# Router, slot table and experts in one block, with expert 0's turned rows from a matrix product

## The chip, the cores and the metric

The kernel runs on one core of a Trainium2 chip. The metric is device time in microseconds of one execution. Engines: PE (TensorE, with PEld for its weight loads), DVE (VectorE), ACT (ScalarE), POOL (GpSimd), SP (SyncE, which here only issues DMAs). All tiles are float32 unless said otherwise.

## The reference, cut to what matters

A first hybrid layer and a second one with latent attention and a recurrence run ahead of the part that matters here, and are not touched. They leave `h`, 512 tokens of 1024 numbers. Then comes a mixture of 32 experts:

```python
logits = (ht @ router_w + router_b)
top_val, top_idx = lax.top_k(logits, TOP_K)            # 4 of 32
gates = jax.nn.softmax(top_val, axis=-1)
# tokens sorted by expert into blocks of 128 slots
u = clamped_swiglu(h_pad[idx] @ w1[e] + b1[e])         # 1024 -> 2048 -> 1024
y = u @ w2[e] + b2[e]                                  # 1024 -> 1024
ffn = sum of a token's 4 rows y, each times its gate
x = layer_norm(DEEPNORM_ALPHA * x + (1 + gt2) * ffn, ln2_g, ln2_b)
```

## The kernel before, in words

The kernel is written engine by engine: a block holds one list of instructions for each engine, the engines meet only at semaphores, and all of them meet at the end of a block. Within an engine the order is that of the code.

`mixed` (L2992) first runs `joined`, which makes `h` (tile `h_mix`, tokens on partitions), stores it to DRAM as `h_rows`, and leaves the router's logits in PSUM bank 6. Then come three blocks.

Block "router" (L3043). POOL clears semaphores, writes zeros and id tiles (L3057 to L3060). SP stores the zeros to the slot table `slot_tokens` in DRAM and issues the first six weight chunks (1 MB each) of expert 0. DVE adds the bias, finds the top four experts of each token, builds a one-hot tile with 16 small comparisons (L3102) and sums it to `member` (L3104). ACT takes the exponentials (L3080). PE counts with 14 products (L3068 to L3071) how many earlier tokens chose the same expert: `rank`. DVE meanwhile weighs the gates (L3107 to L3112). Then (L3115 to L3136) it turns ranks into slot numbers `token_slots`: token of rank r in expert e gets slot 128e + r, and those beyond 128 go to extra blocks. L3139 to L3145 make the plan of these extra blocks.

Block "fill_slots" (L3152). POOL writes token numbers to the slot table with 16 indirect DMAs (L3159), one for each tile of 128 tokens and each choice. PE turns the gates (L3166), ACT makes the diagonals of the last gate (L3172) and copies the turned gates (L3175).

Block "experts" (L3195). For each block of slots POOL's `fetch` (L3329, L3334) loads 128 token numbers and gathers those rows of `h_rows` into `h_mix[:, 0]`. PE turns them (L3363), ACT copies the high part (`high_rows`, L3574) and DVE the low part (`low_rows`, L3481). Weights come in chunks of 128 x 2048, 8 for the first layer and 4 for the second. SP loads them into a ring of six slots; ACT makes the high part (`high`, L3565), DVE the low part (`low`, L3456), PE multiplies (L3382): three products for each piece. From chunk 4 on, `high` waits until PE has used the chunk four before it. SP loads a chunk when `low` has freed its slot. `swiglu` on DVE (L3463 to L3475) and `sigmoid` on ACT (L3569) make `u`. Expert 0's first layer has a part of its own before the loops; PE then turns expert 1's rows and `u`, and the loop over experts 1 to 31 follows, in which the first layer of expert i, the turning of rows i+1 and the second layer of i alternate. SP loads the bias row of the next expert (L3265) between chunks 3 and 4. At the end POOL gathers the four rows of each token, and PE, DVE, ACT and POOL make the output. The extra-block part of each loop is read from the plan with `value_load` after the loop.

Of the kernel before, what the change touches and what calls it, by code (L numbers as in the profile page):

```python
# [13 lines left out]
ALU = mybir.AluOpType  # L14
# [8 lines left out]
P = 128  # L23
SEQ = 512
# [1844 lines left out]
def hybrid_then_moe(nc, A, out):  # L1869
    with ExitStack() as ctx:  # L1870
# [40 lines left out]
        with ExitStack() as inner:  # L1911
            h_rows, slot_tok = mixed(c, A, h, part, inner, gates, slots, plan, vec, gates_T, bias2, gate_diag)
        experts(c, A, h, h_rows, slot_tok, bias_rows, plan, Y, gates, slots, vec, out, gates_T, bias2, gate_diag)


# [1076 lines left out]
def mixed(c, A, h, part, ctx, gates, slots, plan, final, gates_T, bias2, gate_diag):  # L2992

    nc = c.nc

    def sb(name, shape, dt=F32):
        return ctx.enter_context(nc.sbuf_tensor(name, shape, dt))

    h_rows = nc.dram_tensor("h_rows", [SEQ, D], F32).ap()

    slot_tok = nc.dram_tensor("slot_tokens", [SLOTS + CAP, 1], I32).ap()
    hT = sb("hT2", [P, DT, SEQ])
    rw = sb("router_w", [P, DT, E])
    rb = sb("router_b", [P, E])
    c.far.close()
    with nc.sbuf_tensor("leave_rows", [P, 5, D], F32) as vec:
# [10 lines left out]

    logits = sb("logits", [P, TT, E])
    top = sb("top_values", [P, TT, 8])
    top_i = sb("top_indices", [P, TT, 8], U32)  # L3020
    top_f = sb("top_index_f", [P, TT, 8])
    neg = sb("neg_top", [P, TT])
    total = sb("gate_total", [P, TT])
    e_int = sb("expert_ids_i", [P, E], I32)
    e_id = sb("expert_ids", [P, E])
    hot = sb("one_hot", [P, TT, TOPK, E])
    gated_hot = sb("gated_hot", [P, TT, TOPK, E])
    dense = sb("gates_by_expert", [P, TT, E])
    member = sb("member", [P, TT, E])
    rank = sb("rank", [P, TT, E])  # L3030
    count = sb("expert_count", [P, E])
    extra = sb("extra_blocks", [P, 2, E])
    cum = sb("extra_cum", [P, E])
    first = sb("extra_first", [P, E])
    over = sb("over_capacity", [P, TT, E])
    dest = sb("dest", [P, TT, TOPK])
    token_id = sb("token_id", [P, TT], I32)
    blk_i = sb("block_ids_i", [1, EXTRA], I32)
    blk = sb("block_ids", [1, EXTRA])
    before_blk = sb("experts_before", [1, EXTRA, E])  # L3040
    plan_f = sb("plan_f", [1, 2 + EXTRA])
    zeros = sb("zero_ids", [SLOTS // CAP + 1, CAP], I32)
    with nc.Block("router") as block:  # L3043

        @block.sync
        def _(sp):
            sp.wait_ge(c.pool_ready.sem, c.pool_ready.at(1))
            sp.dma_start(slot_tok.rearrange("(b s) o -> b (s o)", s=CAP), zeros[:]).then_inc(c.stored.sem, 16)

            for ch in range(RAW):  # L3050
                load_expert_chunk(c, A, sp, 0, ch)
            sp.wait_ge(c.stored.sem, c.stored.at(1))

        @block.gpsimd
        def _(pool):
            nc.clear_and_free_semaphores(done_with)
            nc.gpsimd.memset(zeros[:], 0)  # L3057
            nc.gpsimd.iota(token_id[:], pattern=[[P, TT]], base=0, channel_multiplier=1)
            nc.gpsimd.iota(blk_i[:], pattern=[[1, EXTRA]], base=0, channel_multiplier=0)
            nc.gpsimd.iota(e_int[:], pattern=[[1, E]], base=0, channel_multiplier=0).then_inc(c.pool_ready.sem, 1)  # L3060

        @block.tensor
        def _(pe):
            pe.wait_ge(c.dve_done.sem, c.dve_done.at(2))
            for t in range(TT):
                out = c.banks[:, 1, t * E:(t + 1) * E]
                for b in range(t):
                    nc.tensor.matmul(out, c.ones[:], member[:, b, :], start=(b == 0), stop=False)  # L3068
                nc.tensor.matmul(out, c.upper_strict[:], member[:, t, :], start=(t == 0), stop=True)
            for b in range(TT):  # L3070
                last = nc.tensor.matmul(c.banks[:, 1, TT * E:(TT + 1) * E], c.ones[:], member[:, b, :], start=(b == 0),  # L3071
                                        stop=(b == TT - 1))
            last.then_inc(c.products.sem, 1)

        @block.scalar
        def _(act):

            act.wait_ge(c.dve_done.sem, c.dve_done.at(1))
            for t in range(TT):
                last = nc.scalar.activation(gates[:, t, :], top[:, t, 0:TOPK], ACT.Exp, bias=neg[:, t:t + 1],  # L3080
                                            accum_out=total[:, t:t + 1])
            last.then_inc(c.act_done.sem, 1)

        @block.vector
        def _(dve):
            dve.wait_ge(c.pool_ready.sem, c.pool_ready.at(1))
            nc.vector.tensor_copy(blk[:], blk_i[:])
            nc.vector.tensor_copy(e_id[:], e_int[:])

            c.dve(dve, nc.vector.tensor_tensor(logits[:], c.banks[:, 6, 0:TT * E].rearrange("p (t e) -> p t e", t=TT),  # L3090
                                               spread(rb[:], TT), ALU.add))
            for t in range(TT):
                last = nc.vector.max(top[:, t, :], logits[:, t, :])
            c.dve(dve, last)
            nc.vector.tensor_scalar(neg[:], top[:, :, 0], -1.0, None, ALU.mult).then_inc(c.dve_done.sem, 1)
            for t in range(TT):
                last = nc.vector.max_index(top_i[:, t, :], top[:, t, :], logits[:, t, :])
            c.dve(dve, last)
            c.dve(dve, nc.vector.tensor_copy(top_f[:], top_i[:]))
            for t in range(TT):  # L3100
                for k in range(TOPK):
                    last = nc.vector.tensor_scalar(hot[:, t, k, :], e_id[:], top_f[:, t, k:k + 1], None, ALU.is_equal)  # L3102
            c.dve(dve, last)
            nc.vector.tensor_reduce(member[:], hot[:].rearrange("p t k e -> p t e k"), AX.X, ALU.add).then_inc(c.dve_done.sem, 1)  # L3104

            dve.wait_ge(c.act_done.sem, c.act_done.at(1))
            c.dve(dve, nc.vector.reciprocal(total[:], total[:]))  # L3107
            c.dve(dve, nc.vector.tensor_tensor(gates[:], gates[:], total[:].unsqueeze(2).broadcast_to([P, TT, TOPK]), ALU.mult))
            c.dve(dve, nc.vector.tensor_tensor(gated_hot[:].rearrange("p t k e -> p (t k) e"), hot[:].rearrange("p t k e -> p (t k) e"),
                                               gates[:].rearrange("p t k -> p (t k)").unsqueeze(2).broadcast_to([P, TT * TOPK, E]),  # L3110
                                               ALU.mult))
            nc.vector.tensor_reduce(dense[:], gated_hot[:].rearrange("p t k e -> p t e k"), AX.X, ALU.add)  # L3112

            dve.wait_ge(c.products.sem, c.products.at(1))
            nc.vector.tensor_copy(rank[:], c.banks[:, 1, 0:TT * E].rearrange("p (t e) -> p t e", t=TT))  # L3115
            c.dve(dve, nc.vector.tensor_copy(count[:], c.banks[:, 1, TT * E:(TT + 1) * E]))

            c.dve(dve, nc.vector.tensor_scalar(extra[:, 0, :], count[:], float(CAP), None, ALU.is_gt))
            for m in range(2, SEQ // CAP):
                c.dve(dve, nc.vector.tensor_scalar(extra[:, 1, :], count[:], float(m * CAP), None, ALU.is_gt))  # L3120
                c.dve(dve, nc.vector.tensor_tensor(extra[:, 0, :], extra[:, 0, :], extra[:, 1, :], ALU.add))
            c.dve(dve, nc.vector.tensor_tensor_scan(cum[:], c.ones[:, 0:E], extra[:, 0, :], 0.0, ALU.mult, ALU.add))
            c.dve(dve, nc.vector.tensor_tensor(first[:], cum[:], extra[:, 0, :], ALU.subtract))

            c.dve(dve, nc.vector.scalar_tensor_tensor(out=first[:], in0=first[:], scalar=float(E - 1), in1=e_id[:],
                                                      op0=ALU.add, op1=ALU.subtract))
            c.dve(dve, nc.vector.tensor_scalar(over[:], rank[:], float(CAP), None, ALU.is_ge))
            c.dve(dve, nc.vector.tensor_tensor(over[:], over[:], spread(first[:], TT), ALU.mult))
            c.dve(dve, nc.vector.tensor_tensor(over[:], over[:], spread(e_id[:], TT), ALU.add))
            c.dve(dve, nc.vector.scalar_tensor_tensor(out=rank[:], in0=over[:], scalar=float(CAP), in1=rank[:],  # L3130
                                                      op0=ALU.mult, op1=ALU.add))
            for k in range(TOPK):
                last = nc.vector.tensor_tensor(hot[:, :, k, :], hot[:, :, k, :], rank[:], ALU.mult)
# [543 lines left out]
```

## Time and profile before

| | us |
|---|---|
| median of 3 runs | 2278.21 |
| the runs | 2267.6, 2278.6, 2278.21 |
| profiled execution, its own time | 2275.14 |
| its span | 2273.5 |
| PE busy | 1981.7 (87%) |
| DVE busy | 1707.6 (75%) |
| ACT busy | 1222.5 (54%) |
| POOL busy | 276.2 (12%) |

The span runs from the first to the last instruction. Busy time is the sum of the durations of an engine's instructions; matmuls overlap their neighbours by their tails, so that eight in a row take less than eight times one. In the timeline a row stands for several instructions of one line; its second column is the time from the first's start to the last's end. The idle time ahead of a row and what ended it stand in brackets. The page divides the span in 40 slices of 57 us: the slices from the nineteenth on belong to the experts' passes.

### The profile page before, as it was taken

The page shows a single profiled execution, that of the slowest core. Times are in us where ns is not written, and L with a number is a line of the kernel's source. Part 1 is how long each engine was busy: PE and PEld are TensorE (multiplying, and loading weights), DVE is VectorE, ACT ScalarE, POOL GpSimd, SP SyncE. Part 2 cuts the span into 40 slices and gives each one's busy share as a digit, 9 for nine tenths or more (in the row PEclk, how much of TensorE's full clock was granted, in tenths as well). Part 3 has the DMA queues.
Part 4 walks back from the last instruction along what each step waited for, and adds up shares of the span by engine and source line. Part 5 has one row for each costly group of instructions (what it writes and reads, how often), then busy time and mean ns, then how long its engine had stood idle before and what let it go on. Part 6 is the DMA issues. An engine that isn't in the chain of part 4 may idle for free.

```text
span 2273.5 us, 26458 instructions
## 1 busy us (share of the span) xinstructions
PE 1981.7 (87%) x9048; PEld 1543.9 (68%) x9048; DVE 1707.6 (75%) x1763; ACT 1222.5 (54%) x1248; POOL 276.2 (12%) x279
## 2 busy tenths in 40 slices
PE   7899887889843994928999999999999999999965
PEld 6666655767523793716878888787888878888751
DVE  5754445844567625837999999999999999999947
ACT  5545554232432121105777776777767777776732
POOL 3436440000001100030000000000000000000012
PEclk9999989999876596957999999999999999999985
DMA  7457415041000102236999999999999999999943
GB/s 207 148 181 235 143 62 180 8 107 47 5 10 5 32 1 103 96 113 243 375 384 369 388 376 380 380 376 386 372 386 376 384 379 371 387 375 386 372 178 144
DMA packets 189694, 537.14 MB, mean 236 GB/s; under 512 B 35954, under 2 KB 59714, under 8 KB 189634
## 3 DMA queue, kind: packets, MB, share of 16 engines
q1 hardware_dynamic: 164930, 461.66, 55.7%
q0 software_dynamic: 18016, 57.91, 7.3%
q10 hardware_dynamic: 6688, 16.79, 1.9%
q8 instruction: 35, 0.57, 0.1%
q14 instruction: 25, 0.20, 0.0%
HBM read 505.97 MB, written 30.33 MB: 236 GB/s over the span
## 4 chain that ended last, share of the span: by engine, by line
PE 51%; DVE 2%; DMA 1%; ACT 1%; issue 0%; POOL 0%; SPq 0%; ACTq 0%; POOLq 0%; DVEq 0%
PE banks L3382 46%; PE banks L3363 2%; PE banks L3368 1%; DMA bias_row<-bias_parts 0%; DVE weights_lo L3456 0%; ACT weights_hi L3565 0%; DVE expert_weights L3521 0%; DMA expert_weights<-slot_outputs,token_slots 0%; DVE x_tokens L3546 0%; DVE out_stats L3531 0%; DVE glu L3521 0%; DMA h_mix<-h_rows,block_tokens 0%; PE banks L3446 0%; PE banks L3447 0%; DVE expert_weights L3526 0%
## 5 line engine op out<-in xcount | busy, mean ns | idle before, releaser
L3456 DVE TENSOR_TENSOR weights_lo<-expert_weights,weights_hi 128x2048 fp32r<-128x2048 f32 x384 | 862.5, 2288 | 50.7 <-ACT weights_hi L3565 50.5
L3565 ACT ACTIVATE weights_hi<-expert_weights 128x2048 fp32r<-128x2048 f32 x384 | 720.2, 1909 | 94.5 <-PE banks L3382 94.5
L3382 PE MATMUL banks<-weights_lo,rows_hi 128*128 128x512 f32 x1024 | 325.3, 399 | 1.8 <-DVE weights_lo L3456 1.8
L3382 PE MATMUL banks<-weights_hi,rows_hi 128*128 128x512 f32 x1024 | 318.2, 392 | 0.0
L3382 PE MATMUL banks<-weights_hi,rows_lo 128*128 128x512 f32 x1024 | 317.3, 391 | 0.0
L3382 PEld LDWEIGHTS banks<-weights_lo,rows_hi 128*128 128x128 f32 x1024 | 188.6, 189 | 65.5 <-DVE weights_lo L3456 15.4
L3382 PEld LDWEIGHTS banks<-weights_hi,rows_hi 128*128 128x128 f32 x1024 | 193.5, 189 | 41.7
L3382 PEld LDWEIGHTS banks<-weights_hi,rows_lo 128*128 128x128 f32 x1024 | 193.4, 189 | 41.6
L3382 PE MATMUL banks<-weights_lo,u_hi 128*128 128x512 f32 x512 | 161.8, 397 | 6.0 <-DVE weights_lo L3456 6.0
L3382 PE MATMUL banks<-weights_hi,u_lo 128*128 128x512 f32 x512 | 158.8, 391 | 0.0
L3382 PE MATMUL banks<-weights_hi,u_hi 128*128 128x512 f32 x512 | 158.6, 391 | 0.0
L3569 ACT ACTIVATE sig<-glu 128x512 f32<-128x512 f32 x64 | 40.5, 632 | 203.6 <-DVE glu L3463 203.6
L3329 POOL DMA_DIRECT2D block_tokens<-slot_tokens x33 | 18.5, 561 | 890.9 <-PE banks L3363 890.6
L892 PE MATMUL banks<-w_in_parts,hnT_parts 128*128 128x512 f32 (+1 forms) x480 | 126.2, 413 | 0.0
L3382 PEld LDWEIGHTS banks<-weights_lo,u_hi 128*128 128x128 f32 x512 | 94.5, 190 | 24.0 <-DVE weights_lo L3456 6.3
L3382 PEld LDWEIGHTS banks<-weights_hi,u_hi 128*128 128x128 f32 x512 | 96.8, 189 | 20.5
L3382 PEld LDWEIGHTS banks<-weights_hi,u_lo 128*128 128x128 f32 x512 | 96.7, 189 | 20.3
L1241 DVE TENSOR_TENSOR w_in_parts<-w_in_landing,w_in_parts 128x1024 fp32r<-128x1024 f32 (+2 forms) x36 | 53.6, 1490 | 73.7 <-ACT w_in_parts L1072 73.5
L892 PEld LDWEIGHTS banks<-w_in_parts,hnT_parts 128*128 128x128 f32 x480 | 93.0, 201 | 21.7 <-issue 6.7
L3363 PE MATMUL banks<-ident,h_mix 128*128 128x128 f32 x520 | 69.1, 277 | 34.2 <-DMA h_mix<-h_rows,block_tokens 30.9
L2043 PE MATMUL banks<-hT_parts,second_parts 128*128 128x512 f32 x336 | 91.1, 423 | 3.8 <-DVE rwkv_raw L2191 3.6
L3363 PEld LDWEIGHTS banks<-ident,h_mix 128*128 128x128 f32 x520 | 61.9, 143 | 43.1 <-issue 34.8
(568 smaller groups left out, 2907.2 us busy)
## 6 DMA issues: line engine op xcount, KB each, us to landing
expert_weights<-in_exp_w SPq DMA_DIRECT2D x384, 1024.0 KB, 8.8
enter_rows<-in_ada_w POOLq DMA_DIRECT2D x24, 1024.0 KB, 5.7
slot_outputs<-h_mix ACTq DMA_DIRECT2D x32, 512.0 KB, 7.0
slot_outputs<-zeros SPq DMA_DIRECT2D x4, 1920.0 KB, 10.5
w_in_landing<-in_w_in SPq DMA_DIRECT2D x16, 384.0 KB, 3.5
second_landing<-in_w_in SPq DMA_DIRECT2D x12, 512.0 KB, 3.7
x_tokens<-in_x SPq DMA_DIRECT2D x8, 512.0 KB, 6.5
w_in_landing<-in_w_in SPq DMA_DIRECT2D x8, 512.0 KB, 3.7
```

Source lines behind the costliest of these rows:

```text
L892: last = nc.tensor.matmul(out, left, right, start=(k == 0 and r == 1), stop=(k == DT - 1 and p == 1))
L1241: v.tensor_tensor(parts[:, n % PLACES, 1, :, 0:w], raw[:, n % RAWS, :, 0:w], parts[:, n % PLACES, 0, :, 0:w], ALU.subtract).then_inc(lo_re ...
L2043: last = nc.tensor.matmul(c.banks[:, b, :], parts[:, n % PLACES, s, kk, tile(b)], hT[:, r, k, :], start=(k == 0 and r == 1), stop=(k == DT ...
L3329: pool.dma_start(ids[:], slot_ids[bass.ds(i, 1), :, :].rearrange("b s o -> (b s) o"), allow_slow_non_contiguous=True).then_inc(ids_in.sem, 16)
L3363: last = nc.tensor.transpose(turned_bank[:, k, :], src[:, k * P:(k + 1) * P], c.ident[:])
L3368: last = nc.tensor.matmul(c.banks[:, bank + n, :], ones[:], row[:, at + n * 512:at + (n + 1) * 512], start=True, stop=False)
L3382: last = nc.tensor.matmul(c.banks[:, bank + n, :], left[:, k, :], right[:, q, kk * FF + n * 512:kk * FF + (n + 1) * 512], start=start, sto ...
L3456: nc.vector.tensor_tensor(w_lo[:, ch % SPLIT, :], c.raw[:, ch % RAW, :], w_hi[:, ch % SPLIT, :], ALU.subtract).then_inc(lo_ready.sem, 1)
L3565: nc.scalar.activation(w_hi[:, ch % SPLIT, :], c.raw[:, ch % RAW, :], ACT.Copy).then_inc(hi_ready.sem, 1)
L3569: nc.scalar.activation(sig[:, half, :], glu[:, half, :], ACT.Sigmoid, scale=SW_ALPHA).then_inc(sig_ready.sem, 1)
```

## The change

The three blocks become one. `mixed` ends after `joined`. The router, the slot table and the gates' tiles move into `experts`, each engine's share at the head of its list. Many of their tiles are now carved out of `glu` and `sig`.

- Expert 0's turned rows no longer come from the slot table. `own_rows` on DVE builds a 0/1 matrix for each of the four token tiles: row = token, column = slot, one where the token is a member of expert 0 and its rank is the column. PE multiplies `h` with it (`first_rows`), which gives the rows of expert 0 turned, in the bank where `turn` used to put them. `fetch(0)` is gone; POOL's fetches begin with expert 1, behind the 16 indirect DMAs.
- The one-hot comparisons become four of 128x128; the counting becomes five products over all tiles at once; two instructions in the chain to the slots are fused.
- DVE: `route`, `weigh`, `own_rows`, `place` (the slots), then `low(0)`, `low_rows(0)`, `low(1)`, `schedule` (the plan), `low(2)` and so on.
- ACT: exponentials, `high(0)`, `high(1)`, `high_rows(0)`, `high(2)`, `high(3)`, the gates' diagonals and turned gates, `high(4)`.
- SP: two weight chunks, then the zeros' store, then the rest. It does not wait for POOL ahead of the first chunks.
- The plan is read behind a new semaphore `planned`.

```diff
 @block.sync
+                for k in range(2):
+                    load_expert_chunk(c, A, sp, 0, k)
+                sp.wait_ge(no_slots_made.sem, 1)
+                sp.dma_start(slot_tok.rearrange("(b s) o -> b (s o)", s=CAP), no_slots[:]).then_inc(no_slots_in.sem, 16)
+                for k in range(2, RAW):
+                    load_expert_chunk(c, A, sp, 0, k)
                 bias_1(0)
 @block.gpsimd
+                nc.clear_and_free_semaphores(done_with)
+                nc.gpsimd.memset(no_slots[:], 0).then_inc(no_slots_made.sem, 1)
+                nc.gpsimd.iota(token_id[:], pattern=[[P, TT]], base=0, channel_multiplier=1)
+                nc.gpsimd.memset(member[:, TT, :], 0.0)
+                nc.gpsimd.iota(id_int[:], pattern=[[1, P]], base=0, channel_multiplier=0).then_inc(ids_made.sem, 1)
                 nc.gpsimd.memset(ones[:], 1.0).then_inc(c.pool_ready.sem, 1)
+                pool.wait_ge(no_slots_in.sem, 16)
+                pool.wait_ge(slots_ready.sem, 1)
+                for t in range(TT):
+                    for k in range(TOPK):
+                        nc.gpsimd.indirect_dma_start(slot_tok, bass.IndirectOffsetOnAxis(slots[:, t, k:k + 1], 0),
+                                                     token_id[:, t:t + 1], None).then_inc(slots_in.sem, 16)
+                pool.wait_ge(slots_in.sem, 16 * TT * TOPK)
...
-                fetch(0)
                 pool.wait_ge(turned_x.sem, 1)
                 fetch(1)
 @block.tensor
+                def count_members():
+                    pe.wait_ge(ids_made.sem, 1)
+                    pe.wait_ge(members.sem, 1)
+                    rows = member[:].rearrange("p t e -> p (t e)")
+                    nc.tensor.matmul(c.banks[:, 1, 0:(TT + 1) * E], c.upper_strict[:], rows, start=True, stop=False)
+                    for b in range(1, TT + 1):
+                        last = nc.tensor.matmul(c.banks[:, 1, b * E:(TT + 1) * E], c.ones[:], rows[:, 0:(TT + 1 - b) * E],
+                                                start=False, stop=(b == TT))
+                    last.then_inc(ranks.sem, 1)
+                def first_rows():
+                    pe.wait_ge(own_hot.sem, 1)
+                    for k in range(DT):
+                        for t in range(TT):
+                            last = nc.tensor.matmul(turned_bank[:, k, :], h[:, t, k * P:(k + 1) * P], own_slots[:, t, :],
+                                                    start=(t == 0), stop=(t == TT - 1))
+                    last.then_inc(turned_x.sem, 1)
...
+                count_members()
+                first_rows()
+                turn_gates()
                 pe.wait_ge(c.pool_ready.sem, c.pool_ready.at(1))
-                pe.wait_ge(rows_in.sem, 16)
-                turn(xg, turned_x)
 @block.vector
+                def own_rows():
+                    dve.wait_ge(ranks.sem, 1)
+                    c.dve(dve, v.tensor_copy(rank[:], c.banks[:, 1, 0:TT * E].rearrange("p (t e) -> p t e", t=TT)))
+                    for t in range(TT):
+                        last = v.tensor_scalar(own_slots[:, t, :], id_row[:], rank[:, t, 0:1], member[:, t, 0:1],
+                                               ALU.is_equal, ALU.mult)
+                    last.then_inc(own_hot.sem, 1)
...
+                route()
+                weigh()
+                own_rows()
+                place()
+                low(0, 0)
                 low_rows(0)
-                for k in range(7):
+                low(1, 1)
+                schedule()
+                for k in range(2, 7):
                     low(k, k)
 @block.scalar
-                high_rows(0)
+                act.wait_ge(maxima.sem, 1)
+                for t in range(TT):
+                    last = nc.scalar.activation(gates[:, t, :], top[:, t, 0:TOPK], ACT.Exp, bias=neg[:, t:t + 1],
+                                                accum_out=total[:, t:t + 1])
+                last.then_inc(exps.sem, 1)
                 for k in range(8):
                     high(k, k, landed(k, 0), k >= SPLIT)
+                    if k == 1:
+                        high_rows(0)
+                    if k == 3:
+                        act.wait_ge(gates_ready.sem, 1)
+                        for t in range(TT):
+                            nc.scalar.activation(gate_diag[:, t, :], c.ident[:], ACT.Copy, scale=gates[:, t, TOPK - 1:TOPK])
+                        act.wait_ge(gates_turned.sem, 1)
+                        nc.scalar.activation(gates_T[:], c.banks[0:E, 7, :], ACT.Copy)
```

## Rows read from the trace of the kernel before

**Rows 1.** One pass: busy us (count) of PE, PEld, DVE, ACT, POOL; clock, DMA, GB/s

```profile
1106.00:1142.00 36.00, 36.00 (x165) 28.86 (x164) 34.34 (x23) 26.22 (x18) 1.53 (x2) 1.00 1.01 381
```

**Rows 2.** List of waits over 30 passes: engine, line, for whom, us in total, times

```profile
ACT weights_hi L3565 <- PE banks L3382: 84.5, 120, 0.8
```

**Rows 3.** PE's timeline: start, us, engine, line, out<-in, count, idle before

```profile
978.39 0.64 PE L3069 MATMUL banks<-member,upper_strict 128*128 128x32 f32 x2 [6.87 <-DVE member L3104]
...
982.68 1.89 PE L3071 MATMUL banks<-member,ones 128*128 128x32 f32 x8
...
1032.67 1.22 PE L3382 MATMUL banks<-weights_lo,rows_hi 128*128 128x512 f32 x2 [1.81 <-DVE weights_lo L3456]
...
1037.92 0.63 PE L3382 MATMUL banks<-weights_lo,rows_hi 128*128 128x512 f32 x2
...
1057.76 1.03 PE L3363 MATMUL banks<-ident,h_mix 128*128 128x128 f32 x8
...
1065.86 1.22 PE L3382 MATMUL banks<-weights_lo,rows_hi 128*128 128x512 f32 x2
```

**Rows 4.** Chain of waits that ended last: start, us, what

```profile
1017.93 2.32 DMA block_tokens<-slot_tokens
...
1025.42 1.95 PE banks L3363 x8
...
1054.75 10.03 DMA bias_row<-bias_parts
```

**Rows 5.** POOL's timeline around the slot table and the fetches

```profile
994.26 1.07 POOL L3159 DMA_INDIRECT slot_tokens<-token_id,token_slots  x1 [21.49 <-DVEq L3152]
...
1013.49 0.97 POOL L3159 DMA_INDIRECT slot_tokens<-token_id,token_slots  x1 [0.30 <-issue]
...
1065.94 1.47 POOL L3334 DMA_INDIRECT h_mix<-h_rows,block_tokens  x1 [5.89 <-DMA block_tokens<-slot_tokens]
```

**Rows 6.** DVE's timeline from the router to expert 0's first layer

```profile
974.85 2.44 DVE L3102 TENSOR_SCALAR one_hot<-expert_ids,top_index_f 128x32 f32<-128x32 f32 x16
...
979.39 1.03 DVE L3112 TENSOR_REDUCE gates_by_expert<-gated_hot 128x128 f32<-128x512 f32 x1
...
988.08 0.90 DVE L3133 TENSOR_TENSOR one_hot<-one_hot,rank 128x128 f32<-128x128 f32 x4
...
989.74 0.17 DVE L3136 CAST token_slots<-dest 128x16 int32<-128x16 f32 x1
...
993.05 0.17 DVE L3145 CAST extra_plan<-plan_f 1x17 int32<-1x17 f32 x1
1028.52 1.23 DVE L3481 TENSOR_TENSOR rows_lo<-banks,rows_hi 128x1024 fp32r<-128x1024 f32 x1 [35.30 <-ACT rows_hi L3574]
...
1049.92 0.69 DVE L3475 TENSOR_TENSOR h_mix<-lin,sig 128x512 f32<-128x512 f32 x1
1050.99 2.29 DVE L3456 TENSOR_TENSOR weights_lo<-expert_weights,weights_hi 128x2048 fp32r<-128x2048 f32 x1 [0.38 <-ACT weights_hi L3565]
```

**Rows 7.** PE's timeline in an earlier stage, f32 products of 128x128

```profile
799.40 1.06 PE L2783 MATMUL banks<-rwkv_room 128*128 128x128 f32 x8
```

**Rows 8.** DVE and POOL side by side, three gathers

```profile
1062.06 8.90 DVE L3456 TENSOR_TENSOR weights_lo<-expert_weights,weights_hi 128x2048 fp32r<-128x2048 f32 x4 [0.15 <-ACT weights_hi L3565]
...
1423.67 4.48 DVE L3456 TENSOR_TENSOR weights_lo<-expert_weights,weights_hi 128x2048 fp32r<-128x2048 f32 x2
...
1423.84 2.96 POOL L3334 DMA_INDIRECT h_mix<-h_rows,block_tokens  x1 [6.45 <-DMA block_tokens<-slot_tokens]
...
1135.57 0.98 POOL L3334 DMA_INDIRECT h_mix<-h_rows,block_tokens  x1 [5.85 <-DMA block_tokens<-slot_tokens]
...
1135.99 4.49 DVE L3456 TENSOR_TENSOR weights_lo<-expert_weights,weights_hi 128x2048 fp32r<-128x2048 f32 x2
```

**Rows 9.** ACT's timeline, gates' diagonal

```profile
993.50 1.28 ACT L3172 ACTIVATE last_gate_diagonal<-ident,gates 128x128 f32<-128x128 f32 x4 [18.28 <-PEq L3043]
```

**Rows 10.** DMA issues, 1059 to 1080: out<-in, engine, op, count, us to landing

```profile
h_mix<-h_rows,block_tokens POOLq DMA_INDIRECT x1, 9.4
```

More of the change, by code:

```diff
@@ L1910, in hybrid_then_moe @@
         gate_diag = ctx.enter_context(nc.sbuf_tensor("last_gate_diagonal", [P, TT, P], F32))
-        with ExitStack() as inner:
-            h_rows, slot_tok = mixed(c, A, h, part, inner, gates, slots, plan, vec, gates_T, bias2, gate_diag)
-        experts(c, A, h, h_rows, slot_tok, bias_rows, plan, Y, gates, slots, vec, out, gates_T, bias2, gate_diag)
+        rb = ctx.enter_context(nc.sbuf_tensor("router_b", [P, E], F32))
+        h_rows, done_with = mixed(c, A, h, part, vec, bias2, rb)
+        experts(c, A, h, h_rows, bias_rows, Y, gates, slots, plan, vec, out, gates_T, bias2, gate_diag, rb, done_with)
 def second_projection(c, A, hT, lat, raw, qT, kT, v_tok, flat, done_with):
@@ L2989, in rwkv_core, with mixed @@
         c.masks.passed(1)
-def mixed(c, A, h, part, ctx, gates, slots, plan, final, gates_T, bias2, gate_diag):
+def mixed(c, A, h, part, final, bias2, rb):
     nc = c.nc
-    def sb(name, shape, dt=F32):
-        return ctx.enter_context(nc.sbuf_tensor(name, shape, dt))
     h_rows = nc.dram_tensor("h_rows", [SEQ, D], F32).ap()
[L3001 to L3006, printed above, removed]
+    with ExitStack() as ctx:
+        hT = ctx.enter_context(nc.sbuf_tensor("hT2", [P, DT, SEQ], F32))
+        rw = ctx.enter_context(nc.sbuf_tensor("router_w", [P, DT, E], F32))
+        c.far.close()
+        vec = ctx.enter_context(nc.sbuf_tensor("leave_rows", [P, 5, D], F32))
         final_rows = [(final[:, 0, :], over_partitions(A["ln2_g_2"].rearrange("a n -> (a n)"), D)),
@@ L3028, in mixed @@
[L3028 to L3133, printed above, removed]
-            c.dve(dve, last)
-            c.dve(dve, nc.vector.tensor_reduce(dest[:], hot[:], AX.X, ALU.add))
-            nc.vector.tensor_copy(slots[:], dest[:])
-            for b in range(EXTRA):
-                last = nc.vector.tensor_scalar(before_blk[:, b, :], cum[0:1, :], blk[:, b:b + 1], None, ALU.is_le)
-            c.dve(dve, last)
-            nc.vector.memset(plan_f[:, 0:1], float(E - 1))
-            nc.vector.tensor_copy(plan_f[:, 1 + EXTRA:2 + EXTRA], cum[0:1, E - 1:E])
-            c.dve(dve, nc.vector.tensor_reduce(plan_f[:, 1:1 + EXTRA], before_blk[:], AX.X, ALU.add))
-            c.dve(dve, nc.vector.tensor_scalar(plan_f[:, 1:1 + EXTRA], plan_f[:, 1:1 + EXTRA], float(E - 1), None, ALU.min))
-            nc.vector.tensor_copy(plan[:], plan_f[:])
@@ L3177, in mixed @@
-    c.products.passed(1)
-    c.gathered.passed(TT * TOPK)
-    return h_rows, slot_tok
+    return h_rows, done_with
 def load_expert_chunk(c, A, engine, e, ch):
@@ L3192, in load_expert_chunk, with experts @@
                      src.rearrange("o p k n -> p (o k) n")).then_inc(c.landed[ch].sem, 16)
-def experts(c, A, h, h_rows, slot_tok, bias_rows, plan, Y, gates, slots, vec, out, gates_T, bias2, gate_diag):
+def experts(c, A, h, h_rows, bias_rows, Y, gates, slots, plan, vec, out, gates_T, bias2, gate_diag, rb, done_with):
     nc = c.nc
@@ L3250, in further @@
                 step(i)
+            engine.wait_ge(planned.sem, 1)
             n = engine.value_load(plan[0:1, 1 + EXTRA:2 + EXTRA], min_val=0, max_val=EXTRA)
@@ L3401, in turn_next_rows @@
                 def turn_next_rows(i, later):
[L3403 removed]
+                    pe.wait_ge(rows_in.sem, 16 + i * 16)
                     if later:
@@ new lines, in schedule @@
+                def schedule():
+                    for b in range(EXTRA):
+                        last = v.tensor_scalar(before_blk[:, b, :], cum[0:1, :], blk[:, b:b + 1], None, ALU.is_le)
+                    c.dve(dve, last)
+                    v.memset(plan_f[:, 0:1], float(E - 1))
+                    v.tensor_copy(plan_f[:, 1 + EXTRA:2 + EXTRA], cum[0:1, E - 1:E])
+                    c.dve(dve, v.tensor_reduce(plan_f[:, 1:1 + EXTRA], before_blk, AX.X, ALU.add))
+                    c.dve(dve, v.tensor_scalar(plan_f[:, 1:1 + EXTRA], plan_f[:, 1:1 + EXTRA], float(E - 1), None, ALU.min))
+                    v.tensor_copy(plan[:], plan_f[:]).then_inc(planned.sem, 1)
```

111 lines of the change are left out of this document (74 added, 37 removed).

## The prediction

> **What bounds the kernel now.** I read the views in the order of the question "what sets the start of the expert passes, and do the passes care". The table by stretch [rows 1] shows one pass (36 us): PE busy 36.00 of 36, at a granted clock of 1.00, DVE 34.34, ACT 26.22. The list of waits over 30 passes [rows 2] has ACT waiting for PE's use of a chunk, 120 times, and no row in which anything waits for a weight chunk to land. So the passes are PE's. Nothing in them is edited, and what the change is worth is how much earlier PE starts expert 1's first product: 1065.86 now [rows 3]. From there to the end the span has 31 loop passes and the tail, as before.
>
> What comes ahead of it is no single engine's work but a chain of small waits. The chain of waits [rows 4] and POOL's timeline [rows 5] show it: slots ready on DVE at 989.91, plan done at 993.22 [rows 6], block change, sixteen DMA_INDIRECT on POOL from 994.26 to 1014.46 (1.27 apart), block change, the fetch of expert 0's rows (ids 2.32, then the gather), turning at 1025.42, first product 1032.67. Between 984.57 and 1025.42 PE only turns the gates.
>
> **The change, part by part.** Times are of the span before, as though the old joined block ended where it ended.
>
> *Route (DVE).* One more memset and a wider iota on POOL put about 0.2 ahead of it. Sixteen TENSOR_SCALAR of 128x32 (2.44) [rows 6] become four TENSOR_TENSOR of 128x128, which as L3133 took 0.90: 1.54 less; a 128x128 cast for two small ones costs 0.1. Members, ready at 978.34, come at 977.1.
>
> *Counting (PE).* 28 records from 978.39 to 984.57 [rows 3], 0.22 each, become 10 (five f32 products, two records each): 2.2, or 3.3 if the 160 to 64 columns wide ones cost more than the 32 wide. I take 2.3: ranks at 979.4. The weighing of the gates on DVE ended 2.1 after the members (980.42) [rows 6] and ends at 979.2 now, so it is hidden under counting. Rank copy 0.3 and four 128x128 TENSOR_SCALAR at 0.23 (four of like size took 0.90): own slots at 980.7.
>
> *The new product (PE).* 8 x 4 = 32 f32 products of 128x128, 64 records. Eight such records took 1.06 with their tail at the full clock [rows 7], 0.11 to 0.13 each; at 1.2 GHz eight transposes of that size took 1.95 with their tail [rows 4] and the counting's records 0.22. I take 0.11 and 0.214. PE is at 1.2 GHz there; after an idle stretch it came up 5.2 us after 1032.67 (a pair of products 1.22, then 0.63) [rows 3]. So 5.3 us at 0.214 is 25 records, 39 more at 0.11 are 4.4: 9.7 us, bounds 7.1 and 13.7. Turned rows stand at 990.4 rather than 1027.37. Copies to high and low part took 2.4 after that (to 1029.75) [rows 6]: 992.8. low(0,0) was done before, between 985.4 and 987.7, so the first product is at 993.8 at the latest, **38.9 earlier**. The transposes of the gates (1 us) lie under those 2.4.
>
> *First layer of expert 0.* PE needed 25.1 (1032.67 to 1057.76) [rows 3]. DVE now has schedule() between low(1) and low(2): 3.3 (989.92 to 993.22) [rows 6]. Lows take 2.23 each (four in 8.90) [rows 8]: low(1) ends 995.1, schedule 998.4, low(2) to low(6) 1000.7 to 1009.7, swiglu 2.8 (four operations of 0.69) [rows 6], low(7) 1015.2, PE's last chunk 2.7 more: 1017.9. PE waits for DVE here, about what the slow clock cost it before, so the layer keeps its length: 24.1. ACT's gate diagonal (1.28) [rows 9] and gates_T stand between high(3) and high(4); they cost nothing, as high(4) comes 4 us before DVE asks for it, and 1.9 on low(4) if that cover goes.
>
> *POOL's queue.* The slots are ready earlier by DVE's savings (989.91 before; from PE's end at 984.57 that was 5.3, of which 0.3 is the rank copy and 0.4 two instructions now fused away; 980.7 and 4.7 is 985.4), and the sixteen DMA_INDIRECT start there and not at 994.26. They used to run beside an idle DVE. Now they run beside the lows, which are TENSOR_TENSOR with both inputs in SBUF. Three rows show what that does: the DMA_INDIRECT at 1423.84, put out 0.17 after a low had begun at 1423.67, took 2.96; the one at 1065.94 took 1.47; the one at 1135.57, beside a rows_lo that reads PSUM, 0.98 [rows 5, 8]. Each of the long ones ends 0.9 after the low that was running ends (1425.91 + 0.9; 1066.51 + 0.9). With 0.3 between two of them, one DMA_INDIRECT goes per low where lows follow one another, and one per 1.27 elsewhere. Followed along DVE's list: number 1 after low(0), 988.6; 2 to 5 by 993.7; 6 after low(1), 996.0; 7 and 8 in schedule(), 998.5; 9 to 13 after low(2) to low(6), 1010.6; 14 and 15 in swiglu, 1013.4; 16 after low(7), **1016.1**. Unhindered it would be 1005.8.
>
> A rule of the Trainium skill goes further than these rows (SBUF — State Buffer, Who interferes with whom): whoever of VectorE and GpSimd starts first has the shared port pair for the whole instruction, and the other blocks. By that rule DVE's low would also wait for a running DMA_INDIRECT. Here the two lows from 1135.99, begun while POOL's ran to 1136.55, took 4.49, as the two from 1423.67 did (4.48) [rows 8]: the trace disagrees for DVE's side, and the sum leaves it out.
>
> *Rows of expert 1.* POOL fetches them after the writes. SP's queue resumes with low(6) and low(7) and puts out five chunks at 1015.2, so all of this meets loaded DMA engines. With idle engines 3.5 went by between the last write's end (1014.46) [rows 5] and the issue of the ids (1017.93) [rows 4], block change included; I take 4.4: 1020.5. Ids 0.3 + 5.9, the idle time ahead of the gather at 1065.94, under load [rows 5]: 1026.7. The gather: at most 5.2 idle (1017.93 + 2.32 to 1025.42) [rows 4], 9.4 loaded [rows 10]; five chunks from 1015.2 are through at about 1029, so 6: rows at **1033.5**, bounds 1029 and 1038. PE finished layer 0 at 1017.9 and waits 15 us for them. From turning them to expert 1's first product 8.1 (1057.76 to 1065.86) [rows 3], in which the clock's loss and the wait for bias_row [rows 4] about cancel: 1041.6 against 1065.86.
>
> *Sum.* **24.2 us earlier**; of the 39 won at expert 0 15 go back to the late rows. What is hidden: no_slots' store, the member memset, `planned` (read 31 passes later). The profiled execution took 2275.1, which gives 2250.9; it lies 3.1 under the median of the three runs (2278.2) and within their spread. I say 2252. About 11 us (0.5%) is what a measurement can tell from no change.
>
> **Rivals.**
> *POOL isn't held* (17%). For it: most gathers take 0.98; against it, the two long ones in rows 5 and 8. Number 16 at 1005.8, quiet fetch 8: rows at 1016, before PE is done. Then bias_row, which needs low(7), sets it: 1015.2 + 11.5 (low(7)'s end 1053.28 [rows 6] to 1064.78 [rows 4]), product at 1027.8: 38 earlier, 2237.
> *DVE is held too* (9%). Seven lows, up to 0.98 each, put low(7) 6.9 later and number 16 with it: product at 1048.6, 17 earlier, 2258. This is how it would go by the rule just cited.
> *POOL gets the port only when DVE rests* (7%). Five writes are done by 993.7, the other eleven start after low(7): 1015.2 + 14.0, rows at 1046.6, product at 1054.7, 11 earlier, 2264. It can't get worse this way, since DVE itself runs out of lows when expert 1's rows are missing. Against it: the long rows end right behind one low, with the next following.
> *It doesn't do what it says* (3%): the early rows free nothing, as PE would wait for bias_row or low(0) all the same. Against it: bias_row(0) and the chunks of low(0) and low(1) are issued ahead of all of this, when the DMA engines have nothing else. Within 0.5% of 2275.
> *The passes get longer* (4%), the slower side. All code is now one block and the tiles lie elsewhere. DVE has 1.66 us to spare in a pass [rows 1]. If each of its 12 lows took 0.26 longer, DVE would have 37.5 and set the pass: 31 x 1.5 = 46 against 24 won, 2297. It decides from 0.8 us a pass on. Nothing in the trace speaks for it.
>
> **The numbers.** Forecast 60%, own range 2246 to 2256 (rows at 1029 to 1038). The range takes in the unheld POOL (2237) and the held DVE (2258), with the few us that executions differ by: 2234 to 2262; left out are the last three cases, 14%. Faster by over 0.5%: 0.60 + 0.17 + 0.09 and a part of the third rival, 0.88. Within 0.5%: the rest of it and the fourth, 0.08. Slower: 0.04.
>
> **What would show it.** Right: turned rows about 37 earlier, 64 records in some 10 us; DMA_INDIRECTs of L3159's kind with durations of 0.98 where DVE is idle and 1.5 to 3 beside lows; PE idle for 10 us or more ahead of the second turning, ended by the gather; passes of 35.96 as before. Wrong: sixteen times 0.97 and no such idle time (first rival); lows of over 2.29 (second); a hole without writes between 993 and 1015 (third); passes over 36 us (last).

## The result, and the profile after

| | before | after |
|---|---|---|
| median of six runs, us | 2278.16 | 2258.1 |
| lowest and highest | 2267.6 to 2279.51 | 2255.43 to 2267.65 |
| profiled execution, span | 2273.5 | 2254.4 |
| expert 1's first product | 1065.86 | 1046.87 |

The ratio is 0.993 (95% interval 0.9902 to 0.9958): the kernel became 16 to 20 us faster. 2252 with a move of 26 had been forecast, and 2234 to 2262 as the range: the time lies within it and the move fell short.

The passes did not change. The table by stretch, one pass, columns as in [rows 1]:

```profile
1106.00:1142.00 36.00, 36.00 (x166) 28.91 (x165) 34.27 (x23) 26.37 (x18) 1.54 (x2) 1.00 1.01 382
```

PE's timeline, which answers to [rows 3]:

```profile
977.00 0.87 PE L3301 MATMUL banks<-member,upper_strict 128*128 128x160 f32 x2 [5.46 <-DVE member L3406]
...
980.95 9.94 PE L3312 MATMUL banks<-sig,h_mix 128*128 128x128 f32 x64 [1.54 <-DVE sig L3423]
...
1001.20 0.73 PE L3254 MATMUL banks<-weights_lo,rows_hi 128*128 128x512 f32 x2 [1.63 <-DVE weights_lo L3355]
...
1039.61 1.97 PE L3235 MATMUL banks<-ident,h_mix 128*128 128x128 f32 x8 [21.01 <-DMA h_mix<-h_rows,block_tokens]
...
1045.91 1.03 PE L3240 MATMUL banks<-bias_row,ones_bf 3*128 3x512 bf16 x2
```

The 64 records of the product (its 0/1 matrix lies in `sig`) run from 980.95 and take 9.94. PE is through with expert 0's first layer at 1018.6 and stands 21 us for expert 1's rows. DVE's timeline, where [rows 6] had the router, the plan and the lows:

```profile
985.31 0.17 DVE L3448 CAST token_slots<-dest 128x16 int32<-128x16 f32 x1
...
993.13 2.28 DVE L3355 TENSOR_TENSOR weights_lo<-expert_weights,weights_hi 128x2048 fp32r<-128x2048 f32 x1
...
998.79 0.17 DVE L3459 CAST extra_plan<-plan_f 1x17 int32<-1x17 f32 x1
998.87 11.08 DVE L3355 TENSOR_TENSOR weights_lo<-expert_weights,weights_hi 128x2048 fp32r<-128x2048 f32 x5
...
1013.07 2.29 DVE L3355 TENSOR_TENSOR weights_lo<-expert_weights,weights_hi 128x2048 fp32r<-128x2048 f32 x1 [0.39 <-ACT weights_hi L3546]
```

And POOL's, which answers to [rows 5]:

```profile
986.39 2.24 POOL L3196 DMA_INDIRECT slot_tokens<-token_id,token_slots  x1 [13.43 <-DVE token_slots L3448]
...
994.07 2.19 POOL L3196 DMA_INDIRECT slot_tokens<-token_id,token_slots  x1 [0.30 <-issue]
...
999.09 11.71 POOL L3196 DMA_INDIRECT slot_tokens<-token_id,token_slots  x1 [0.31 <-issue]
1011.10 0.96 POOL L3196 DMA_INDIRECT slot_tokens<-token_id,token_slots  x1 [0.30 <-issue]
...
1020.32 1.24 POOL L3196 DMA_INDIRECT slot_tokens<-token_id,token_slots  x1 [0.30 <-issue]
1028.46 0.57 POOL L3202 DMA_DIRECT2D block_tokens<-slot_tokens  x1 [6.90 <-DMA slot_tokens<-token_id,token_slots]
1035.24 0.99 POOL L3207 DMA_INDIRECT h_mix<-h_rows,block_tokens  x1 [6.20 <-DMA block_tokens<-slot_tokens]
```

Read the two side by side. A write beside an idle DVE or DVE's small operations takes some 0.97; those beside a single low take 2.2 to 2.4. The ninth starts 0.22 after low(2) and lasts 11.71: it ends at 1010.80, 0.85 after the *fifth* low of the row above. In the kernel before, no DMA_INDIRECT read for the forecast had been held past one low. The last row but one shows the second delay: the last write is over at 1021.56, and its landing is awaited until 1028.2. The share of DMA time from 985 to 1045, and the issues in it (count, KB each, median us to landing):

```profile
DMA  9999940737930000069726899998898997370000
...
slot_tokens<-token_id,token_slots POOLq DMA_INDIRECT x16, 6.6
block_tokens<-slot_tokens POOLq DMA_DIRECT2D x2, 0.5 KB, 4.1
```

A write to the slot table took 2.1 to land in the kernel before, by the same view.

### The profile page after: what moved, and what is told of

It reads as the page before. It is cut to its first block, busy times and chain, and to the rows that moved or that the text cites. A ratio compares the mean times of both kernels' runs of the same rounds, so it can differ in the third digit from the quotient of the medians.

```text
span 2254.4 us, 26466 instructions
## 1 busy us (share of the span) xinstructions
PE 1982.9 (88%) x9086; PEld 1546.8 (69%) x9086; DVE 1706.4 (76%) x1752; ACT 1226.0 (54%) x1248; POOL 284.8 (13%) x277
## 4 chain that ended last, share of the span: by engine, by line
PE 51%; DVE 2%; POOL 1%; DMA 1%; issue 1%; ACT 0%; ACTq 0%; POOLq 0%; DVEq 0%
PE banks L3254 46%; PE banks L3235 3%; PE banks L3240 1%; POOL slot_tokens L3196 1%; DMA slot_tokens<-token_id,token_slots 0%; DVE expert_weights L3502 0%; DMA expert_weights<-slot_outputs,token_slots 0%; DMA block_tokens<-slot_tokens 0%; DVE x_tokens L3527 0%; DVE out_stats L3512 0%; DVE glu L3502 0%; DMA h_mix<-h_rows,block_tokens 0%; PE banks L3345 0%; PE banks L3346 0%; DVE expert_weights L3509 0%
## 5 line engine op out<-in xcount | busy, mean ns | idle before, releaser
L1241 DVE TENSOR_TENSOR w_in_parts<-w_in_landing,w_in_parts 128x1024 fp32r<-128x1024 f32 (+2 forms) x36 | 53.6, 1489 | 73.2 <-ACT w_in_parts L1072 73.1
L892 PE MATMUL banks<-hnT_parts,w_in_parts 128*128 128x512 f32 x336 | 84.8, 405 | 3.8 <-DVE hnT_parts L1446 3.8
```

The source lines that it names most:

```text
L892: last = nc.tensor.matmul(out, left, right, start=(k == 0 and r == 1), stop=(k == DT - 1 and p == 1))
L1241: v.tensor_tensor(parts[:, n % PLACES, 1, :, 0:w], raw[:, n % RAWS, :, 0:w], parts[:, n % PLACES, 0, :, 0:w], ALU.subtract).then_inc(lo_re ...
```

## The experiments

**The measure.** Where the router begins shifts by up to 9.3 us from profile to profile (DVE's first cast there at 966.96 to 976.27), before anything that the kernels differ in. From the start of expert 1's bias matmul on PE to the end of the span it is 1207.4 to 1210.4 us in every profile, also of before. So each kernel is judged by the **stretch** between the two: 1064.90 - 972.80 = 92.1 in the kernel before, 1045.91 - 972.85 = 73.1 in the changed one, 19.0 less. Times of runs stand beside it.

Theory at the start: the lows hold POOL's writes, and late writes make late rows. Rivals: the product or the block's merging brings less than thought; loaded DMA engines alone make the rows late.

**POOL's signal ahead of low(2).** The changed kernel, with

```diff
+                pool.sem_inc(written.sem, 1)
...
                 schedule()
+                dve.wait_ge(written.sem, 1)
                 for k in range(2, 7):
```

> DVE waits, ahead of low(2) of expert 0, until POOL has issued all sixteen slot writes. Measured by the time at which PE starts expert 1's first product (before 1065.86, changed kernel 1046.87). Theory (a DMA_INDIRECT doesn't get through while DVE runs instructions with two SBUF inputs without a gap): writes nine to sixteen take 0.97 each, the last ends near 1009, PE's first layer of expert 0 gets about 10 us longer and ends near 1028, rows of expert 1 are there before that, product at 1037: 10 us earlier than the changed kernel. Rival (the ninth write waits for room in the DMA queue, or for landed writes, whatever DVE does): one write of over 5 us remains, and DVE's wait only adds its length: 1047 or later.

The signal did not hold DVE: low(2) began at 1002.28, right behind the plan, with half of the writes to come. POOL's sequencer had run ahead of them. Yet the writes beside the lows changed:

```profile
1002.50 2.91 POOL L3197 DMA_INDIRECT slot_tokens<-token_id,token_slots  x1 [0.30 <-issue]
1005.72 1.90 POOL L3197 DMA_INDIRECT slot_tokens<-token_id,token_slots  x1 [0.30 <-issue]
```

One goes at the end of each low now. Stretch 68.5; 2253.84 us, ratio 0.9906 (0.9884 to 0.9928). The test missed its aim and showed something else: with a wait that was met at once, the long hold was gone.

**A pause behind each low.** A memset of one element, and the wait for it, after each of low(2) to low(6):

```diff
                 for k in range(2, 7):
                     low(k, k)
+                    c.dve(dve, v.memset(pause[:, k:k + 1], 0.0))
```

> A memset of one number on DVE, waited for, behind each of low(2) to low(6) of expert 0, about 0.2 us each. Theory as in my prediction (a write gets through at each end of a low, if DVE leaves a gap): one write per low, the last ends near 1015 rather than 1021.6, rows and expert 1's product 6 us earlier, 1041. If the port is given up only when DVE rests for long: no change, the ninth write takes 11 to 12 us. Rival (room in the DMA queue): no change either, 1047 plus 1.

The writes beside these lows take 2.90, 2.04, 2.05, 2.05 and 2.04; stretch 68.5; 2252.25 us, ratio 0.9909 (0.9886 to 0.9932). That is the same as with one wait.

**Lows with one input from PSUM.** low(1) to low(6) subtract a PSUM bank instead of the high part: same length and count, but the low parts of these six chunks are left out of the result.

```diff
+                def low_other(ch, s):
...
+                                            c.banks[:, 6, :].unsqueeze(1).broadcast_to([P, 4, 512]),
...
-                    low(k, k)
+                    low_other(k, k)
```

> low(1) to low(6) of expert 0 take their second input from PSUM instead of SBUF, in the same size and order, so that they have one SBUF input; the low parts of these chunks are left out by it. Theory: writes beside these lows take 0.97 like alone (the first, beside low(0), still 2.2, and those beside swiglu and low(7) up to 3), the last ends near 1008, expert 1's rows by 1019, and its product follows from PE's own end and bias_row: 1026 to 1029, 18 to 20 us earlier than the changed kernel. Rival (room in the queue, loaded DMA engines): the ninth write stays at 11 us and the product at 1047.

```profile
997.75 6.66 DVE L3470 TENSOR_TENSOR weights_lo<-expert_weights,banks 128x2048 fp32r<-128x2048 f32 x3
...
1005.90 0.97 POOL L3196 DMA_INDIRECT slot_tokens<-token_id,token_slots  x1 [0.30 <-issue]
1008.41 0.57 POOL L3202 DMA_DIRECT2D block_tokens<-slot_tokens  x1 [1.54 <-DMA slot_tokens<-token_id,token_slots]
```

Three of those lows follow one another in 6.66, as fast as before, and the writes beside them take 0.96 or 0.97. Of the others only the first, beside low(0), takes more than 1.01. The hold comes from the lows' two SBUF inputs: neither room in the queue nor loaded DMA engines can be its cause, since the same writes are put out and the DMA engines move 0.96 MB from 998 to 1002, against 0.94 in the changed kernel. The last write is over at 1006.87, the rows are there before PE asks, and the stretch is 58.7, 14.4 less; one run, 2241.38 us. The edit has a side effect: ACT makes the high part of chunk 5 only at 1006.58, DVE then stands 4.12 ahead of the fourth of these lows, and expert 0's layer ends 51.7 after the first cast instead of 45.8. Why ACT is late there is not shown. So 14.4 is a rough price of the hold and the late fetch together, rather too low than too high, since the layer itself ended later.

**One block, but no product.** POOL fetches expert 0's rows and PE turns them, as before the change; all else is the changed kernel.

```diff
-                first_rows()
...
+                pe.wait_ge(rows_in.sem, 16)
+                turn(xg, turned_x)
```

> The change without its title part: one block, but expert 0's rows are fetched by the slot table and turned, as before. Theory: DVE has only low(0) beside the slot writes, so the last ends near 1007 instead of 1014.5, expert 0's rows come some 7 to 9 us earlier than before and so does expert 1's product: 1057 to 1059. The rest of the 19 us (about 11) is the product's. Rival (merging the blocks is what brings the gain, since block ends cost 3 us each and SP, ACT and DVE start earlier): 1047 to 1050 here too.

Stretch 81.3; 2265.31 us, ratio 0.9953 (0.9932 to 0.9974). So 10.8 of the 19.0 come without the product, from the merged block and the shorter chain to the slots, and 8.2 from the product. Here the writes behind the first two take 0.97, since DVE has nothing to do while they run: the product starts the lows, and the lows hold the writes. The lows come later, when POOL stands idle:

```profile
1026.23 11.08 DVE L3357 TENSOR_TENSOR weights_lo<-expert_weights,weights_hi 128x2048 fp32r<-128x2048 f32 x5
```

They take the same 11.08 as beside the held write of the changed kernel.

**DVE waits for the written table.** DVE stands ahead of low(2) until all 16 writes have landed.

```diff
+                dve.wait_ge(slots_in.sem, 16 * TT * TOPK)
                 for k in range(2, 7):
```

> In e1 the signal of POOL came as soon as its queue was filled, not when the writes were made, so DVE was not held. Here DVE waits, ahead of low(2), for the semaphore of all sixteen landed writes. Theory (two SBUF inputs on DVE hold a DMA_INDIRECT): no write beside a low from the seventh on, all 0.97, last one ends near 1009, low(2) starts near 1011, low(7) ends near 1027.5, PE ends expert 0's first layer near 1030, rows of expert 1 are there by 1018 and no longer matter, its product follows from bias_row at 1039: 8 us earlier than in the changed kernel (1046.9), 3 earlier than e2 with its start set off. Rival (rows late by the queue): a write of over 5 us remains, product after 1047.

```profile
1010.80 0.57 POOL L3202 DMA_DIRECT2D block_tokens<-slot_tokens  x1 [1.46 <-DMA slot_tokens<-token_id,token_slots]
...
1012.89 1.22 PE L3254 MATMUL banks<-weights_lo,rows_hi 128*128 128x512 f32 x2 [14.21 <-DVE weights_lo L3355]
```

PE loses 14.2 in the middle of expert 0's first layer, which ends at about 1033 rather than 1018.6, and the kernel still gains: stretch 67.1, 2249.72 us, ratio 0.9869 (0.9848 to 0.9889). Landing took 1.5 and the ids 2.5, close to the 2.6 of the kernel before; no weights were being loaded then. Standing idle for the table costs less than working beside it as the changed kernel does. It gains no more, though, than ending the long hold alone (68.5 above).

**Expert 1's rows from a product too.** A second 0/1 matrix (in `lin`) and 64 more records, into banks 6 and 7; POOL's first fetch is expert 2's.

```diff
-                first_rows()
+                first_rows(0, turned_bank, own_slots)
+                first_rows(1, second_bank, next_slots)
...
-                turn_next_rows(0, False)
```

> Expert 1's turned rows also come from a product with a 0/1 matrix, right behind the first one, in banks 6 and 7; POOL's first fetch is that of expert 2; the turned gates move to bank 4. Theory (all that the changed kernel gave back was the wait for expert 1's rows): PE does 64 records more, 7 us, at about 991 to 998, the first layer of expert 0 ends near 1020.5, no turning of rows between the layers, expert 1's first product at 1028.5 from bias_row's landing or from PE itself: 18 us earlier than the changed kernel, about 2239 in all. The held writes stay held and no longer matter. Rival (something else, such as the loaded DMA engines or bias_row, would take its place): 1040 or later, less than 7 us gained.

```profile
991.64 7.31 PE L3312 MATMUL banks<-lin,h_mix 128*128 128x128 f32 x64
...
1000.06 5.10 POOL L3198 DMA_INDIRECT slot_tokens<-token_id,token_slots  x1 [0.30 <-issue]
...
1030.98 1.02 PE L3240 MATMUL banks<-bias_row,ones_bf 3*128 3x512 bf16 x2 [2.86 <-DMA bias_row<-bias_parts]
```

Stretch 56.6; 2238.34 us, ratio 0.9818 (0.9791 to 0.9846). The writes are still held (5.10 through two lows, then 2.4 to 2.6 each beside the next three), but nobody waits for them. The median is the lowest of the study.

**The plan earlier.** `schedule()` right behind low(0), where DVE waits for the turned rows anyway.

```diff
                 low(0, 0)
+                schedule()
                 low_rows(0)
                 low(1, 1)
-                schedule()
```

> schedule() moves up to the time in which DVE waits for the high part of the rows (behind low(0)), so that PE needn't wait for low(2). Theory (POOL's writes set the end): expert 0's first layer ends up to 2 us earlier, but low(1) to low(6) now run without a break and hold the writes longer, product of expert 1 unchanged or up to 2 us later, 1046 to 1049. Rival (DVE's own work sets it): 3 us earlier.

```profile
992.12 1.22 DVE L3380 TENSOR_TENSOR rows_lo<-banks,rows_hi 128x1024 fp32r<-128x1024 f32 x1 [0.53 <-ACT rows_hi L3555]
993.26 13.50 DVE L3355 TENSOR_TENSOR weights_lo<-expert_weights,weights_hi 128x2048 fp32r<-128x2048 f32 x6
...
996.69 1.90 POOL L3196 DMA_INDIRECT slot_tokens<-token_id,token_slots  x1 [0.30 <-issue]
```

A miss of both: the stretch is 66.7 (one run, 2248.98 us), though the lows now follow one another without a gap, six in 13.50. The writes beside them take 1.9 to 2.1 each; the long hold is gone.

**The changed kernel again.** No edit: does the long hold come back?

> The changed kernel as it is, profiled once more. If the hold of the ninth write through five lows (11.7 us) is how the two engines always meet there, it comes again, and expert 1's product again lies 19 us ahead of before. If it is chance, the writes take 2 to 3 us each as in e1, and the product comes some 4 to 5 us earlier, as in e1 and e2.

```profile
992.56 11.71 POOL L3196 DMA_INDIRECT slot_tokens<-token_id,token_slots  x1 [0.30 <-issue]
```

It does, now of the eighth write and just as long. Stretch 73.3; 2254.29 us, ratio 0.9893 (0.987 to 0.9916). So it is no accident of one execution, and it goes with the row of lows behind the plan and not with which write it is.

**A wait that is already met.** One line on the changed kernel; the value it waits for was reached 13 us before.

```diff
                 schedule()
+                dve.wait_ge(slots_ready.sem, 1)
                 for k in range(2, 7):
```

> The changed kernel, and DVE waits ahead of low(2) for a semaphore that has long had its value (slots_ready at 1). Nothing else differs. If the long hold of POOL's write (11.7 us through five lows, in both profiles of the changed kernel) comes from the lows following schedule without any wait between, the writes beside low(2) to low(6) now go one per low, 1.9 to 2.9 us each, and the stretch from the first router cast to expert 1's bias matmul is 68.5 us, as in the run with POOL's signal. If it was POOL's extra instruction there that made the difference, one write is held 11.7 us again and the stretch is 73 us.

```profile
998.43 2.92 POOL L3196 DMA_INDIRECT slot_tokens<-token_id,token_slots  x1 [0.30 <-issue]
1001.66 1.90 POOL L3196 DMA_INDIRECT slot_tokens<-token_id,token_slots  x1 [0.30 <-issue]
...
998.22 11.10 DVE L3355 TENSOR_TENSOR weights_lo<-expert_weights,weights_hi 128x2048 fp32r<-128x2048 f32 x5
```

The lows start when they did (0.09 after the start of the plan's last cast, 0.08 in the changed kernel) and take 11.10 rather than 11.08, and one write goes per low. The sixteenth is over at 1015.56, 43.4 after the first cast; forecast were 43.3, measured in the changed kernel 48.7. Stretch 68.2, 4.9 less; 2253.33 us, ratio 0.9917 (0.9892 to 0.9943). The stretch shows the gain; the runs are too few to tell 5 us from the changed kernel's.

**Two products, the plan earlier, bias ahead.** The kernel with two products, with `schedule()` behind low(0), and expert 1's bias row loaded ahead of its chunks:

```diff
+                sp.wait_ge(b1_used.sem, 1)
+                bias_1(1)
...
-                    if k == 4:
-                        sp.wait_ge(b1_used.sem, 1)
-                        bias_1(1)
```

> Two products, with two more things: the drawing up of the next layer's sums (schedule) stands right behind low(0) on DVE, and SP loads expert 1's bias ahead of expert 1's weight chunks. Measured from DVE's first router cast to the start of expert 1's bias matmul, the kernel with two products took 56.6 us, of which PE waited 2.86 for that bias. If what stood after the second product was the bias and DVE's start of the lows, the stretch is now 52 to 54 us, and the kernel 3 to 4 us faster than with two products alone, about 2235 us. Rival: DVE's low rows still set the start of the first product, and the bias only hid it: the stretch stays at 55 to 56.5 and the time within 1.5 us of 2238.

```profile
995.43 1.20 DVE L3380 TENSOR_TENSOR rows_lo<-banks,rows_hi 128x1024 fp32r<-128x1024 f32 x1
996.57 6.67 DVE L3355 TENSOR_TENSOR weights_lo<-expert_weights,weights_hi 128x2048 fp32r<-128x2048 f32 x3
...
997.23 6.86 POOL L3197 DMA_INDIRECT slot_tokens<-token_id,token_slots  x1 [0.30 <-issue]
...
1029.26 1.06 PE L3234 MATMUL banks<-ident,h_mix 128*128 128x128 f32 x8 [4.13 <-DVE rows_lo L3380]
1030.25 0.88 PE L3239 MATMUL banks<-bias_row,ones_bf 3*128 3x512 bf16 x2
```

The wait for the bias is gone and the stretch is 54.0, at the upper end of what was expected. The time is not: 2241.08 us, ratio 0.985 (0.9825 to 0.9876), which can't be told from the kernel with two products. What is left there is PE's 4.13 for DVE's low rows, which stood in the kernel with two products as well. The long hold is back, 6.86 through three lows, though the plan stands where it stood in the kernel with the plan moved alone, in which no write was held past one low. A difference on DVE: there it stood idle for 0.53 between the plan and the low rows, and here it went straight through. No run changed that idle time alone.

## Why the prediction was right in kind and wrong in two terms

**Right: what sets the time, and all steps to the end of expert 0's layer.** Members came at 976.9 (forecast 977.1), ranks at 979.4, the product's start at 980.95 (980.7), its length 9.94 (9.7), turned rows at 990.9 (990.4), first product 993.8 (993.8), slots ready 985.5 (985.4), low(7) done 1015.4 (1015.2), layer done 1018.6 (1017.9). The weighing of the gates stayed under the counting. PE's granted clock was 0.50 from 980 to 985 and 0.89 from 985 to 991, so the product ran in two parts as reckoned; in the other runs it took 9.11 to 10.19. PE's clock loss and DVE's plan about cancelled: the layer took 24.6 (24.1 forecast, 25.1 before).

**Right: where the gain is given back.** PE waits for expert 1's rows, because the writes run beside the lows; the run with PSUM inputs shows this cause, since there the wait is gone.

**Wrong: "one DMA_INDIRECT goes per low".** It was read from two gathers that were each held to the end of one low (the third ran beside an instruction that reads PSUM), and applied to five lows behind the plan. One of the two, at 1065.94, even had more lows right behind its own; but that row of lows began after 0.15 of idle time on DVE, and the row behind the plan after none. The ninth write was held through all five, and number 16 ended at 1021.56 instead of 1016.1, 5.5 late. The run with the met wait has the forecast's pattern and its sixteenth write, and comes close to its 1041.6: in the changed kernel's time its first product would stand at 1046.87 - 4.9 = 1042.0.

**Wrong in size: the landing of the last write.** The ids were issued 6.9 after it instead of 4.4, 2.5 more. The load was foreseen, its price was not: the only row at hand was of idle DMA engines. Where no weights were being loaded the landing was awaited 1.5 in each of three runs, and where they were, 5.8 to 7.0; no run changed the load alone. The gap to the gather was 6.8 for 6.2; from its issue to the turning 4.4 passed for 6.8; from the turning to the product 7.3 for 8.1. The sum of the misses, 5.5 + 2.5 + 0.6 - 2.4 - 0.8 = 5.4, is the 5.3 by which the first product came late. The gather and the steps behind it had been taken 3.2 too long together; it is luck that this hid a part of the other misses. By the profiles 24.2 was forecast and 19.0 measured; the medians' 26 and 20 are the same difference with what runs differ by on top.

**The rivals.** An unheld POOL is excluded by the trace (and would have been worth some 14 more, as the run with PSUM inputs shows; 38 was forecast for it and 33.4 measured there). A held DVE is excluded as well, though its forecast of 2258 is what the kernel happens to measure. By the rule cited in the prediction (Trainium skill, SBUF — State Buffer, Who interferes with whom) the engine that issues first has the shared ports for its whole instruction and the other is blocked. The section says this of VectorE's modes that use two ports; of an instruction with two SBUF inputs it says that it contends with GpSimd's reads. That POOL is blocked the trace bears out, and goes beyond one instruction, with 11.71 for 0.97. For DVE it disagrees again: the five lows took 11.08 beside a DMA_INDIRECT that was under way nearly all the while, and 11.08 with POOL idle in the run without the product. "POOL only when DVE rests" had been given 7%; in the changed kernel it was true for this one row of lows, and the writes did not stay back until low(7), as it had them. The passes kept their 36.00, and the rival on the slower side found nothing.

## What to carry to other kernels

Moving a queue of GpSimd's indirect DMAs under VectorE work with two SBUF inputs is no free overlap: count how many such instructions follow each other without a pause, not how many there are, and look for one row that shows the whole pattern. Where the result of small indirect writes is needed soon, try to let them land before the large loads resume; here even letting VectorE stand for them was better than the changed kernel (stretch 67.1, against 73.1 and 73.3), though no better than one more wait ahead of the lows (68.2) or the plan moved (66.7). And if a matrix product can replace the first table-driven gather, the second gather may be the next to go: here that took 16.4 off the stretch, where the whole change had taken 19.0.

## What the runs showed of the hardware that was not expected

- A DMA_INDIRECT of POOL was held through five TENSOR_TENSOR with two SBUF inputs (11.71, twice), through three (6.86) and two (5.10), where DVE went from the plan's small operations to them with neither idle time nor a separate wait. Each low carries a wait of its own, for the high part; that one does not help. With one more wait, met long before, it was 2.92 and then 1.90 each. With an idle stretch of 0.53 behind the plan it was 1.9 to 2.1 each. What inside the engine makes the difference stays open: the condition fits every profile here, but no run varied the idle time alone.
- The lows themselves did not lengthen: five took 11.08 beside the held write and 11.08 with POOL idle.
- POOL's increment behind 16 DMA_INDIRECTs reached DVE with at least eight of them still to run. It says that they are queued, not that they are done.
- The landing of the last small write was awaited 1.5 where no weights were being loaded, and 5.8 to 7.0 where they were; the ids took 2.5 to 2.6 and 5.2 to 7.2.
